# The opening of a two-block fp32 kernel: the input loaded in four pieces, scaled in token order, rounded from the transposes' banks

## What is computed

```python
def rmsnorm(x, g):
    x32 = x.astype(jnp.float32)
    y = x32 * lax.rsqrt(jnp.mean(x32 * x32, axis=-1, keepdims=True) + EPS)
    return (y * g.astype(jnp.float32)).astype(x.dtype)

def rglru_layer(x, norm_g, w_in, conv_w, conv_b, wr, br, wi, bi, lam, w_out):
    h = rmsnorm(x, norm_g)
    u = h @ w_in
    xb, gate = u[..., :LRU_WIDTH], u[..., LRU_WIDTH:]
    xb = causal_depthwise_conv(xb, conv_w, conv_b)
    ...
    return x + y @ w_out
```

## Time and profile before

| | |
|---|---|
| median of 3 runs | 838.84 us (838.83 to 838.92) |
| the profiled execution's own time | 838.82 us |
| its span in the trace | 837.0 us (1.82 us lie outside it) |
| TensorE busy | 806.7 us, 96% |
| VectorE busy | 551.7 us, 66% |
| ScalarE busy | 468.7 us, 56% |
| GpSimd busy | 124.9 us, 15% |
| granted TensorE clock, mean | 0.995 of full speed |

### The profile page before, as it was taken

One profiled execution on the slowest core, in us unless ns is written; L12 is line 12 of the kernel. 1 busy time (PEld: TensorE's weight loads), 2 busy tenths in 40 slices (PEclk: granted clock), 3 DMA queues, 4 the chain that ended last, 5 costly groups with the idle time before them and its releaser, 6 DMA issues.

```text
span 837.0 us, 16462 instructions
## 1 busy us (share of the span) xinstructions
PE 806.7 (96%) x6371; PEld 775.1 (93%) x6371; DVE 551.7 (66%) x811; ACT 468.7 (56%) x732; POOL 124.9 (15%) x143
## 2 busy tenths in 40 slices
PE   5999799999899999999999999999999999999997
PEld 5999799897699999999999999998999999999885
DVE  6987995867658766666448755455577766666443
ACT  5679844767856544454345455655747454444433
POOL 9315620215503000000003003000001200000000
PEclk9999899999999999999999999999999999999999
DMA  8624347462236666655655544443545666665651
GB/s 257 211 76 130 122 152 228 128 192 89 95 95 208 202 184 189 180 177 181 193 176 154 179 147 143 134 126 122 179 134 183 192 200 189 186 176 179 181 193 50
DMA packets 104104, 136.35 MB, mean 163 GB/s; under 512 B 5049, under 2 KB 92529, under 8 KB 104049
## 3 DMA queue, kind: packets, MB, share of 16 engines
q1 hardware_dynamic: 102288, 133.26, 51.9%
q0 software_dynamic: 1600, 2.28, 1.0%
q10 hardware_dynamic: 160, 0.05, 0.0%
HBM read 134.51 MB, written 1.05 MB: 162 GB/s over the span
## 4 chain that ended last, share of the span: by engine, by line
PE 74%; ACT 4%; DVE 4%; POOL 3%; issue 1%; POOLq 0%; ACTq 0%; DVEq 0%
PE bank L480 54%; PE bank L540 7%; PE bank L488 7%; POOL arena L432 2%; ACT a_hi L933 2%; DVE w_lo L1373 1%; PE bank L719 1%; ACT w_hi L933 1%; ACT arena L933 1%; PE bank L738 1%; PE bank L731 1%; PE bank L896 1%; DVE arena L1677 1%; PE bank L884 1%; DVE a_lo L1408 0%
## 5 line engine op out<-in xcount | busy, mean ns | idle before, releaser
L480 PE MATMUL bank<-a_hi,w_hi 128*128 128x256 f32 (+1 forms) x1672 | 477.8, 286 | 11.1 <-DVE w_lo L1373 6.2
L480 PE MATMUL bank<-a_lo,w_hi 128*128 128x256 f32 (+1 forms) x1672 | 473.9, 283 | 0.0
L480 PE MATMUL bank<-a_hi,w_lo 128*128 128x256 f32 (+1 forms) x1672 | 473.7, 283 | 0.0
L1373 DVE TENSOR_TENSOR w_lo<-stage,w_hi 128x1024 fp32r<-128x1024 f32 x250 | 317.8, 1280 | 223.0 <-ACT w_hi L933 222.8
L933 ACT ACTIVATE w_hi<-stage 128x1024 fp32r<-128x1024 f32 x250 | 260.6, 1052 | 160.6 <-PE bank L480 115.0
L480 PEld LDWEIGHTS bank<-a_hi,w_hi 128*128 128x128 f32 x1672 | 321.5, 192 | 15.5 <-issue 7.9
L480 PEld LDWEIGHTS bank<-a_lo,w_hi 128*128 128x128 f32 x1672 | 321.7, 192 | 0.0
L480 PEld LDWEIGHTS bank<-a_hi,w_lo 128*128 128x128 f32 x1672 | 321.6, 192 | 0.0
L933 ACT ACTIVATE arena<-arena 128x512 f32<-128x512 f32 (+4 forms) x63 | 37.8, 605 | 76.1 <-DVE arena L1440 42.9
L432 POOL TENSOR_TENSOR arena<-arena 128x512 f32<-128x512 f32 x12 | 23.0, 1925 | 375.1 <-ACT arena L933 374.8
L488 PE MATMUL bank<-w_hi,a_hi 128*128 128x256 f32 x208 | 60.5, 291 | 1.7 <-DVE a_lo L1408 1.7
(11 more groups left out here) (178 smaller groups left out, 670.2 us busy)
## 6 DMA issues: line engine op xcount, KB each, us to landing
stage<-ffn_w_gate SPq DMA_DIRECT2D x44, 512.0 KB, 3.8
stage<-ffn_w_up SPq DMA_DIRECT2D x44, 512.0 KB, 3.8
stage<-ffn_w_down SPq DMA_DIRECT2D x44, 512.0 KB, 3.6
stage<-w_in SPq DMA_DIRECT2D x40, 512.0 KB, 3.5
stage<-a_w_in SPq DMA_DIRECT2D x24, 512.0 KB, 4.8
stage<-b_w_in SPq DMA_DIRECT2D x16, 512.0 KB, 4.0
stage<-a_w_out SPq DMA_DIRECT2D x12, 512.0 KB, 3.8
stage<-b_w_out SPq DMA_DIRECT2D x8, 512.0 KB, 3.6
```

The costliest lines, as they stand in the source:

```text
L480: mm = pe.matmul(dst, w[:, slot, c:c + P], a[:, k, :] if isinstance(k, int) else wide(a[:, bass.ds(k, 1), :]), start=start and n == 0, sto ...
L1373: dve.tensor_tensor(w_lo[:, n % RING, 0:w], src, w_hi[:, n % RING, 0:w].bitcast(F32), ALU.subtract)\
```

## The change

The input `x` is loaded first, in four pieces of 128 tokens by 512 features, each with its own semaphore. The identity and the gain rows move from SP's queue to ScalarE's; the five `rows_a` loads move from ScalarE's queue to SP's, behind the first two chunks of weights. Each piece is squared and summed when it lands. The reciprocals are then applied to `x` in token order (`rooted_x(j)`: ScalarE the first 128 tokens, VectorE the other 128, in pieces of 256 features), the scaled `x` is transposed a second time (`turn_ahead(k)`, two transposes into bank 5, 6 or 7 for each tile k), and ScalarE and VectorE take high and low part straight from that bank, with the gain as a factor. `roots(0, 6)`, `spread` and the eight writes `normalised(k)` are gone. The 16 transposes of the unscaled `x` stay, ahead of the new ones. The first half chunk of weights is split and rounded in two pieces of 512 columns (`w_first`). All four `input_out` copies now come behind the last rounding of `x` and behind `hi(2)`. The block `if c == 0` above is as before.

```diff
+        x_tok = tiles(12, 8).rearrange("p (b d) -> p b d", b=TB)
+        x_rst = tiles(XNF, 8).rearrange("p (b d) -> p b d", b=TB)
...
-            sp.dma_start(ident, I["constants"][:, IDENT:IDENT + P]).then_inc(id_in, 16)
-            sp.dma_start(rows_n[:, :], I["a_norm_g"].rearrange("o (k p) -> (o k) p", p=P)).then_inc(rows_n_in, 16)
             xt = I["x"].rearrange("o (b p) d -> p (o b) d", p=P)
-            sp.dma_start(tiles(0, 8).rearrange("p (b d) -> p b d", b=TB), xt).then_inc(x_in, 16)
+            for q, (h, tb) in enumerate(X_PIECES):
+                sp.dma_start(x_tok[:, tb, h * 512:(h + 1) * 512], xt[:, tb, h * 512:(h + 1) * 512]).then_inc(x_in[q], 16)
...
-            stream(C_X, 6, lambda j: col(w_in, j))
+            load(C_X, col(w_in, 0))
+            load(C_X + 1, col(w_in, 1))
+            for first, name, n in ((CONV_B, "a_conv_b", LT), (BR, "a_gate_r_b", LT), (BI, "a_gate_i_b", LT),
+                                   (LAM, "a_lambda", LT)):
+                sp.dma_start(rows_a[first:first + n, :], I[name].rearrange("o (k p) -> (o k) p", p=P))\
+                    .then_inc(rows_a_in, 16)
+            sp.dma_start(rows_a[CONV_W:CONV_W + CONV * LT, :],
+                         I["a_conv_w"].rearrange("o c (k p) -> (o c k) p", p=P)).then_inc(rows_a_in, 16)
+            for j in range(2, 6):
+                load(C_X + j, col(w_in, j), split(C_X + j - 2))
...
+            def turn_ahead(k):
+                pe.wait_ge(xs_a, k // 2 + 1)
+                pe.wait_ge(xs_d, k // 2 + 1)
+                if k >= 3:
+                    pe.wait_ge(xl_ready, k - 2)
+                if k == 2:
+                    pe.wait_ge(par_ready, 1)
+                for tb in range(TB):
+                    mm = pe.transpose(bank[5 + k % 3][:, tb * P:(tb + 1) * P], x_rst[:, tb, k * P:(k + 1) * P], ident)
+                mm.then_inc(xt_done, 1)
...
-                pe.wait_ge(w_done, half + 1 if ready is None else ready)
+                if chunk == C_X and h == 0:
+                    pe.wait_ge(w_first, 1)
+                else:
+                    pe.wait_ge(w_done, half + 1 if ready is None else ready)
...
+                    if chunk == C_X:
+                        if k == 2:
+                            pe.wait_ge(w_done, 1)
+                        if k < KD - 2:
+                            turn_ahead(k + 2)
...
-            pe.transpose(bank[5][:, 0:KD], rows_n[:, :], con[0:KD, IDENT:IDENT + KD]).then_inc(par_t, 1)
-            pe.wait_ge(x_in, 16)
-            xtok = tiles(0, 8).rearrange("p (b d) -> p b d", b=TB)
-            for m in range(KD):
-                for tb in range(TB):
+            pe.transpose(bank[7][:, 0:KD], rows_n[:, :], con[0:KD, IDENT:IDENT + KD]).then_inc(par_t, 1)
+            for q, (h, tb) in enumerate(X_PIECES):
+                pe.wait_ge(x_in[q], 16)
+                for m in range(4 * h, 4 * h + 4):
                     c = (m % 2) * T + tb * P
-                    mm = pe.transpose(bank[m // 2][:, c:c + P], xtok[:, tb, m * P:(m + 1) * P], ident)
-                if m % 2:
-                    mm.then_inc(acc_done, 1)
-                if m == 3:
-                    roots(0, 6)
+                    mm = pe.transpose(bank[m // 2][:, c:c + P], x_tok[:, tb, m * P:(m + 1) * P], ident)
+                    if tb == 1 and m % 2:
+                        mm.then_inc(acc_done, 1)
+            turn_ahead(0)
+            turn_ahead(1)
...
-            act.wait_ge(rows_n_in, 16)
...
+            act.dma_start(ident, I["constants"][:, IDENT:IDENT + P]).then_inc(id_in, 16)
+            act.dma_start(rows_n[:, :], I["a_norm_g"].rearrange("o (k p) -> (o k) p", p=P)).then_inc(rows_n_in, 16)
+            for h in range(2):
+                act.wait_ge(x_in[2 * h], 16)
+                f(tiles(SQ + 2 * h, 2), x_tok[:, 0, h * 512:(h + 1) * 512], ACT.Square, accum_out=x_ms[:, h, 0:1])\
...
             act.wait_ge(ms_ready, 2)
...
+            def rooted_x(j):
+                f(x_rst[:, 0, j * T:(j + 1) * T], x_tok[:, 0, j * T:(j + 1) * T], ACT.Identity, scale=n_rstd[:, 0:1])\
+                    .then_inc(xs_a, 1)
...
-                act.wait_ge(xn_ready, k + 1)
-                f(a_hi[:, k, :], tiles(XNF + k), ACT.Copy).then_inc(xh_ready, 1)
+                act.wait_ge(xt_done, k + 1)
+                f(a_hi[:, k, :], bank[5 + k % 3][:, 0:T], ACT.Identity, scale=GAINS[0][:, k:k + 1]).then_inc(xh_ready, 1)
...
             def input_out(b):
+                act.wait_ge(acc_done, b + 1)
                 f(wide(xres[:, 2 * b:2 * b + 2, :]), bank[b][:, :], ACT.Copy).then_inc(x_ready, 1)
...
-            hi(0)
-            for k in range(KD):
+            act.wait_ge(rstd_ready, 1)
+            rooted_x(0)
+            act.wait_ge(par_ready, 1)
+            normalised_hi(0)
+            act.wait_ge(stage_in[0], 16)
+            f(w_hi[:, 0, 0:2 * T], stage[:, 0, 0, 0:2 * T], ACT.Copy).then_inc(w_first_hi, 1)
+            rooted_x(1)
+            normalised_hi(1)
+            f(w_hi[:, 0, 2 * T:HALF], stage[:, 0, 0, 2 * T:HALF], ACT.Copy).then_inc(hi_done, 1)
+            rooted_x(2)
+            normalised_hi(2)
+            normalised_hi(3)
+            hi(1)
+            rooted_x(3)
+            for k in range(4, KD):
                 normalised_hi(k)
-                if k == 1:
-                    hi(1)
-                if k == 5:
-                    hi(2)
-                if k in (3, 4, 6, 7):
-                    input_out((3, 4, 6, 7).index(k))
+            hi(2)
+            for b in range(4):
+                input_out(b)
             hi(3)
...
-            dve.wait_ge(x_in, 16)
-            dve.tensor_tensor_reduce(tiles(SQ + 4, 4), tiles(4, 4), tiles(4, 4), 1.0, 0.0, ALU.mult, ALU.add,
-                                     accum_out=n_ms[:, 1:2]).then_inc(ms_ready, 1)
...
+            for h in range(2):
+                dve.wait_ge(x_in[2 * h + 1], 16)
+                x = x_tok[:, 1, h * 512:(h + 1) * 512]
+                dve.tensor_tensor_reduce(tiles(SQ + 4 + 2 * h, 2), x, x, 1.0, 0.0, ALU.mult, ALU.add,
+                                         accum_out=x_ms[:, h, 1:2]).then_inc(x_sq, 1)
+                if h == 0:
+                    dve.wait_ge(par_t, 1)
+                    dve.tensor_copy(par_n[:, :], bank[7][:, 0:KD]).then_inc(par_ready, 1)
+            dve.wait_ge(x_sq, 4)
+            dve.tensor_tensor(n_ms[:, :], x_ms[:, 0, :], x_ms[:, 1, :], ALU.add).then_inc(ms_ready, 2)
             root_inv(0)
...
-            def normalised(k):
...
-                dve.wait_ge(acc_done, k // 2 + 1)
-                dve.scalar_tensor_tensor(tiles(XNF + k), bank[k // 2][:, (k % 2) * T:(k % 2 + 1) * T], GAINS[0][:, k:k + 1],
-                                         spread[:, :], ALU.mult, ALU.mult).then_inc(xn_ready, 1)
...
+            def rooted_x(j):
...
+                dve.tensor_scalar(x_rst[:, 1, j * T:(j + 1) * T], x_tok[:, 1, j * T:(j + 1) * T], n_rstd[:, 1:2], 1.0,
+                                  ALU.mult, ALU.mult).then_inc(xs_d, 1)
...
             def normalised_lo(k):
                 dve.wait_ge(xh_ready, k + 1)
-                low(k, tiles(XNF + k), 1).then_inc(xl_ready, 1)
...
-            lo(0)
-            roots_out(0, 6)
-            normalised(0)
-            normalised(1)
+                dve.scalar_tensor_tensor(a_lo[:, k, :], bank[5 + k % 3][:, 0:T], GAINS[0][:, k:k + 1],
+                                         a_hi[:, k, :].bitcast(F32), ALU.mult, ALU.subtract).then_inc(xl_ready, 1)
+            for j in range(4):
+                rooted_x(j)
             normalised_lo(0)
-            normalised(2)
+            dve.wait_ge(w_first_hi, 1)
+            dve.tensor_tensor(w_lo[:, 0, 0:2 * T], stage[:, 0, 0, 0:2 * T], w_hi[:, 0, 0:2 * T].bitcast(F32), ALU.subtract)\
+                .then_inc(w_first, 1)
             normalised_lo(1)
-            normalised(3)
+            dve.wait_ge(hi_done, 1)
+            dve.tensor_tensor(w_lo[:, 0, 2 * T:HALF], stage[:, 0, 0, 2 * T:HALF], w_hi[:, 0, 2 * T:HALF].bitcast(F32),
+                              ALU.subtract).then_inc(w_done, 1)
             normalised_lo(2)
-            normalised(4)
             normalised_lo(3)
-            normalised(5)
             lo(1)
-            normalised_lo(4)
-            normalised(6)
-            normalised_lo(5)
-            normalised(7)
-            normalised_lo(6)
-            normalised_lo(7)
+            for k in range(4, KD):
+                normalised_lo(k)
             lo(2)
             lo(3)
```

26 lines of the change are left out of this document (11 added, 15 removed).

## The result

The changed kernel takes **842.07 us** (median of 6 runs, 840.97 to 843.03); the kernel before took 838.84 (838.70 to 838.94, 6 runs beside them). The ratio is 1.0038, 95% interval [1.0027, 1.0048]: slower by 3.2 us. The forecast was 839.1 with a range from 838.0 to 841.9, so the time lies just outside it, on the side to which I had given 0.23, and well beyond the 1.7 us that I had counted as no change.

What follows compares the result with a forecast made beforehand. TensorE, busy 806.7 of 837.0 us, was taken to bound the kernel, so chunk 1's start sets the time. Chunk 1 at 20.2 against 19.88 gave +0.3: span 837.3 plus 1.82 outside, 839.1 us, range 838.0 to 841.9.

Steps and rivals of the forecast that it cites:

- the side to which I had given 0.23: Whole kernel: measurably slower, by more than 1.7 us, from late gain rows or the low clock; chance 0.23.
- The yardstick: Start of chunk 1 on TensorE: its gain or loss passes on one for one while the stretch to 92.00 stays closed.
- The forecast of that start, 20.2: Chunk 1 on TensorE would start at 20.2 us, against 19.88 before: +0.3 us.
- the last quarter of `x`: Input load: the last of the four pieces would land at 5.7 us, with 256 KB taking 0.69 us.
- TensorE's pace: Rival: TensorE stays at the low clock in chunk 0's first half and the transposes, +1.5 to +2.1 us; chance 0.08.
- the other condition: Before `turn_ahead(0)`: scaled `x` would be ready at 7.7 us, so TensorE's own order would rule.
- the 14th instruction: TensorE's opening: some 14 instructions would run at the slow 0.21 us step, later ones at 0.11.
- R: Opening: time at which TensorE gets going, once the gain rows are in; taken as 4.7 us, range 3.1 to 5.7.
- The rival of late gain rows: Opening: ScalarE's loads sit behind SP's transfers; R of 7.6 to 8.6 gives +3.2 to +4.2 us; chance 0.19.
- The new wait behind chunk 0: Before the parameter transpose: TensorE waits 1.3 us for ScalarE's four `input_out` copies.
- The margin in front of chunk 2: Taps would end at 25.6 and chunk 2 need them at 25.9; the margin falls from 0.9 to about 0.3 us.
- the start of `turn_ahead(0)`: TensorE's opening: after handover, gain rows and sixteen old transposes, 3.2 us from R, it would begin at 8.35 us.

Runs made afterwards that it cites:

- the combined kernel: Changed kernel with `x` in one load, squares in one instruction per engine, 12 and 8 constant matmuls, unscaled transposes behind `turn_ahead(1)`, copies in ScalarE's gaps: 838.78 us.
- the third run of the first round: Changed kernel with identity and gain rows moved back to the head of SP's queue, ahead of the four pieces of `x`: 843.31 us.
- best version: The combined kernel with 11 and 5 constant matmuls, unscaled transposes first, roundings and copies reordered, parameter rows turned into bank 7: 837.24 us, ratio to the kernel before 0.9983.

## Why the prediction was wrong

**Which step failed.** The yardstick held: all of the loss stands at the start of chunk 1, and the stretch to 92 us stayed closed. The forecast of that start, 20.2, was 2.8 us too early, in two terms: the last quarter of `x`, worth 0.7 of it, and TensorE's pace, worth 2.1.

*The last quarter of `x`, 5.7; measured 6.89.* I priced four pieces like one transfer, at the 374 GB/s of the earlier trace rows. While they land the traffic is lower, 250 to 354 GB/s in windows of half a microsecond from 3.5 to 6.5 us, with weights among it (the kernel before has 358 to 426 from 4.0 to 6.5). Two of these windows of the changed kernel (length, granted clock, DMA share, GB/s):

```profile
5.50:6.00 0.50, 1.00 0.76 252
6.00:6.50 0.50, 1.00 0.81 250
```

The DMA engines have idle time in them. The late piece shifted the reciprocal from an end at 7.2 to one at 8.47 and the scaled `x` from 7.7 to 9.0, so that the other condition, not TensorE's order, ruled `turn_ahead(0)`: 9.06 for 8.35, +0.7 us. The 0.7 is read from this trace; by itself the cost of the pieces is shown only in the kernel before, where it is 2.1 us. No run gives it in the changed kernel, since the one with a single load had its gain from the pace. The change sets out to have `x` earlier; by its pieces it lost what the earlier issue had won. The Trainium skill (DMA: Bandwidth & Descriptors, "Measured (HBM→SBUF, 128 partitions, SWDGE, issued from GpSimd)") has a rule for this that I passed over, to make transfers of 1 MB or more; it stands there beside figures for loads that GpSimd issues, while these are issued by SP. The traces agree for quarters; halves lost only 0.25 to 0.55 us, so here the bound isn't sharp.

*TensorE's pace, a rival at 0.08.* This is the step that failed most. I let the low pace end with the 14th instruction, as before. It lasted until 17.3 us. From `turn_ahead(0)` to chunk 0 it took 2.90 us and not 2.45, and chunk 0 took 9.2 us from first to last matmul and not 7.5: +2.1 together. With the 0.7 above, and 0.1 less at the end, that is the 2.8. The same kernel with constant matmuls has 2.50 and 7.42 in these two places, and the combined kernel with and without them puts the pace at 1.98 us: both at or close to the +1.5 to +2.1 that I had given to this rival. The mechanism was there with its price; the chance was wrong. What I took for evidence against it, a gap of 1.73 us before 12.46 that did no harm, came in the kernel before after 16 transposes and four matmuls without a pause, from 6.7 to 10.7, the last of them at full pace already. In the changed kernel TensorE also works without a pause, from 4.60 to 8.47, then waits 0.59 and 1.44 us, and is slow all the same. What decides it isn't settled. The run with the copies in the gaps has the same work up to there, but went over to the full pace at 9.31 and, behind a wait of 1.65, back to the low one; the one with a single load worked from 6.43 to 10.6, waited 1.65 too and then had the full pace. Shown is only that added work in these gaps raises it. The Trainium skill (TensorE: Matmul & The Clock Gate, "HAM oscillation — how this bites in real kernels") warns that waits between short bursts of matmuls can put TensorE back to the low clock each time; the waits in its example are longer than the bursts. The traces agree for longer waits: after 2.53 us in the kernel before with 11 constant matmuls, and after 4.55 in the one with the weights held back, the matmuls went 0.21 apart. Whether the rule covers the 0.59 and 1.44 here, no run shows.

**What was right.** R was 4.60 for 4.7: the issue of the identity stands at 0.78, while the table load ran from 0.74 to 2.02, so a load is issued behind a running table load. The Trainium skill (Perfetto Trace Analysis, the lifecycle of a DVE / Act instruction) has it so, and the trace agrees. ScalarE's packets moved while `x` was on its way: from 2.4 to 3.4 us its queue served 115 packets beside 113 of SP's:

```profile
q1 hardware_dynamic: 113, 0.21, 72.6%
q10 hardware_dynamic: 115, 0.05, 29.0%
```

The rival of late gain rows was thus refuted; the third run of the first round shows that earlier rows win nothing. The new wait behind chunk 0 was 1.40 for 1.3, and its cause is as given. The margin in front of chunk 2 sufficed, but barely: the taps ended at 28.69, and the chunk's first matmul is at 28.81. Here my sum had a slip that stayed without effect: from `par_a` to the end of the taps the old rows have 3.85 us (20.83 to 24.68), so 22.0 leads to 25.85 and not 25.6. The terms I give for the start of `turn_ahead(0)` add up to 8.25, not 8.35.

**What stays open.** Some executions of these kernels have one more low stretch of TensorE's clock near 216 to 222 us. Three profiled executions have it (one load, combined without constant matmuls, best version), and in each the span, against that of the kernel before, is 1.5 us longer than the start of chunk 1 accounts for. By their times, three in ten of the best version, four in nine with the 16 constant matmuls and three in nine with the copies in the gaps are in such an upper heap, and so is the kernel before: 12 of the 84 executions beside the batches took 840.3 to 840.5 us, though none of those was profiled. So the changed kernels don't have it alone; some have it more often. The profiled execution of the changed kernel has no such stretch, so its 3.1 us are the opening's alone. Whether the spread of its six runs (840.97 to 843.03) comes from this is open: their mean clocks (0.993 to 0.996) don't go with their times. A delay of chunk 1 as such doesn't bring it. What decides it isn't settled. Nor is how the engines divide their time between the pieces and the weights behind them.

## What to carry to other kernels

Cutting a load so that work can start on its first part can make the last part later, and where a result needs the whole (a root over all features) only the last part counts: read when the last piece lands, with what is queued behind it. Before a dense stretch is moved forward, look at what TensorE does in the microseconds ahead of it; it may go at half its pace into that stretch (here for 5.3 us of it), and the time is then lost in every matmul and not in a wait that the profile would name. And where a wait in front of a dense stretch is only for a buffer, as bank 3 was for the parameter rows, another buffer takes the wait away: in the best version the transpose of the parameter rows (18.07) follows the last matmul of chunk 0 at once.

## What the runs showed of the hardware

- Four transfers of 256 KB issued one behind the other completed 1 MB at 8.80 us where one transfer did at 6.65; with the next loads held back 7.48; in pieces of 64 partitions 9.20, with windows of 170 to 240 GB/s from 4.0 to 8.5; in two transfers 6.9 and 7.2.
- The low pace with which TensorE starts isn't in the column of the granted clock: it reads 1.00 from 12 to 17 us in the changed kernel while the instructions are 0.21 us apart, as at a record of 0.50 near 101 us. Later falls are in it: 0.51 from 13.5 to 16.9 in the kernel before with 11 constant matmuls, 0.50 from 16.5 to 18 with the weights held back, 0.51 from 12.0 to 15.4 with the copies in the gaps. In an opening the spacing of the instructions has to be read, not that column.
- TensorE's pace falls again after short idle times at full pace: with constant matmuls from 1.0 to 6.0 us and a wait of 2.5 us before 12.58, the matmuls were 0.21 apart from 13.5 to 16.9, nearly a microsecond after they had begun at 0.12. With a wait of 1.65 us before 11.60 it fell at 12.0 in one execution (copies in the gaps); with a wait of 1.65 before 12.27 it didn't in another (one load).
